# A mixture-of-experts stage whose narrow expert passes take fp32 weights unsplit, on the two column halves of the array

## What is computed

```python
def swiglu(h, w_gate, w_up, w_down):
    return (jax.nn.silu(h @ w_gate) * (h @ w_up)) @ w_down

def moe_swiglu(h, router_w, w_gate, w_up, w_down):
    logits = (h @ router_w).astype(jnp.float32)
    top_val, top_idx = lax.top_k(logits, TOP_K)
    top_w = jax.nn.softmax(top_val, axis=-1)
    gates = jnp.sum(jax.nn.one_hot(top_idx, N_EXPERTS, dtype=jnp.float32) * top_w[..., None], axis=-2)
    y = jnp.zeros_like(h)
    for e in range(N_EXPERTS):
        y = y + gates[..., e:e + 1] * swiglu(h, w_gate[e], w_up[e], w_down[e])
    return y
```

## Time and profile before

| | us |
|---|---|
| median of 3 runs | 1770.15 |
| lowest and highest | 1768.28, 1770.39 |
| profiled execution, first to last instruction (span) | 1766.1 |
| expert stage up to the M passes, from the first narrow product to the first M product | 745 to 1494 |
| M passes and end | 1494 to 1766 |

### The profile page before, as it was taken

The page is one execution under the profiler, slowest core; times in us unless marked ns, Lnnn a source line. Parts: engine busy times, 40 slices in busy tenths (PEclk is TensorE's granted clock), DMA queues, the critical chain, the costliest instruction groups (busy, mean ns, idle before and its releaser), DMA issues.

```text
span 1766.1 us, 25732 instructions
## 1 busy us (share of the span) xinstructions
PE 1692.1 (96%) x9921; PEld 1375.2 (78%) x9921; DVE 1364.1 (77%) x1225; ACT 1095.0 (62%) x1091; POOL 50.4 (3%) x100
## 2 busy tenths in 40 slices
PE   6999999899999999999899999999999999999997
PEld 4999999699999786667677776777677766788785
DVE  5666767576677687598698979897978888887886
ACT  2445544543333556587676877676867768767774
POOL 0200000001011000000000000000000000000000
PEclk9999999999999999899999999999999999999999
DMA  9975655268788440299799989998999899999993
GB/s 349 336 262 199 215 203 199 76 226 297 263 297 297 143 143 25 96 360 368 271 330 379 345 309 381 343 381 303 386 336 363 311 354 381 371 354 337 365 351 129
DMA packets 245612, 504.89 MB, mean 286 GB/s; under 512 B 11360, under 2 KB 83200, under 8 KB 245504
## 3 DMA queue, kind: packets, MB, share of 16 engines
q1 hardware_dynamic: 230224, 458.26, 72.1%
q0 software_dynamic: 12032, 43.00, 6.7%
q10 hardware_dynamic: 3248, 2.17, 0.4%
HBM read 502.34 MB, written 1.05 MB: 285 GB/s over the span
## 4 chain that ended last, share of the span: by engine, by line
PE 70%; DVE 16%; issue 7%; ACT 4%; DMA 1%; ACTq 0%; DVEq 0%; SPq 0%
PE ps L1410 18%; PE ps L1414 12%; DVE wlo L1618 10%; PE ps L1007 9%; PE ps L1011 9%; PE ps L1014 9%; PE ps L1458 3%; ACT whi L606 2%; PE ps L1388 2%; PE ps L1503 2%; PE ps L1062 1%; PE ps L1156 1%; PE ps L1180 1%; PE ps L1100 1%; DMA raw<-mod_w 1%
## 5 line engine op out<-in xcount | busy, mean ns | idle before, releaser
L1618 DVE TENSOR_TENSOR wlo<-raw,whi 128x2048 fp32r<-128x2048 f32 x428 | 967.8, 2288 | 245.9 <-ACT whi L606 241.0
L606 ACT ACTIVATE whi<-raw 128x2048 fp32r<-128x2048 f32 x428 | 807.8, 1913 | 196.1 <-PE ps L1011 81.9
L1410 PE MATMUL ps<-whi,ahi 128*128 128x512 f32 x896 | 297.7, 408 | 2.4 <-issue 1.8
L1414 PE MATMUL ps<-wlo,ahi 128*64 128x512 f32 (+1 forms) x896 | 259.0, 396 | 19.7 <-DVE wlo L1618 19.6
L1007 PE MATMUL ps<-ahi,whi 128*128 128x256 f32 x832 | 238.6, 287 | 1.7 <-DVE alo L1686 1.7
L1011 PE MATMUL ps<-alo,whi 128*128 128x256 f32 x832 | 235.8, 283 | 0.0
L1014 PE MATMUL ps<-ahi,wlo 128*128 128x256 f32 x832 | 235.7, 283 | 0.0
L1414 PEld LDWEIGHTS ps<-wlo,ahi 128*64 128x64 f32 (+1 forms) x896 | 136.5, 155 | 94.5 <-DVE wlo L1618 33.8
L1410 PEld LDWEIGHTS ps<-whi,ahi 128*128 128x128 f32 x896 | 165.9, 190 | 47.7 <-issue 11.2
L1007 PEld LDWEIGHTS ps<-ahi,whi 128*128 128x128 f32 x832 | 159.9, 192 | 5.1 <-issue 3.8
L1011 PEld LDWEIGHTS ps<-alo,whi 128*128 128x128 f32 x832 | 159.9, 192 | 0.3
(11 more groups left out here) (263 smaller groups left out, 2112.9 us busy)
## 6 DMA issues: line engine op xcount, KB each, us to landing
raw<-l_exp_w_gate SPq DMA_DIRECT2D x112, 1024.0 KB, 7.4
raw<-l_exp_w_up SPq DMA_DIRECT2D x112, 1024.0 KB, 7.9
raw<-l_exp_w_down SPq DMA_DIRECT2D x112, 1024.0 KB, 6.9
raw<-l_w_in SPq DMA_DIRECT2D x42, 1024.0 KB, 6.1
mraw<-mod_w POOLq DMA_DIRECT2D x80, 512.0 KB, 5.3
raw<-l_ffn_w_gate SPq DMA_DIRECT2D x14, 1024.0 KB, 5.1
raw<-l_ffn_w_up SPq DMA_DIRECT2D x14, 1024.0 KB, 6.5
raw<-l_ffn_w_down SPq DMA_DIRECT2D x14, 1024.0 KB, 5.7
```

Source lines behind the costliest of these rows:

```text
L606: act.activation(whi[s % SPL][:, :], raw[s % RAW][:, :], ACT.Copy).then_inc(hi_done, 1)
L1410: ins = pe.matmul(dst, stat, whi[s % SPL][:, a:a + BANK], start=start, stop=False, skip_group_check=True)
L1414: ins = pe.matmul(dst, stat, wlo[s % SPL][:, a:a + BANK], start=False, stop=stop, skip_group_check=True)
L1618: dve.tensor_tensor(wlo[s % SPL][:, :], raw[s % RAW][:, :], whi[s % SPL][:, :].bitcast(F32), ALU.subtract).then_inc(lo_done, 1)
```

## The change

Narrow passes stop splitting their weights. `as_landed` names the tiles of the narrow passes (`WHOLE`): all four gate and up tiles of a narrow step, and its two down tiles. `high` and `low` return at once for these tiles, and the numbering of split tiles (`split_at`) leaves them out.

- TensorE reads such a tile straight from `raw`, in fp32, with an fp32 stationary of 64 columns. `gate_beside_up` puts gate on columns and partitions 0 to 63 and up on 64 to 127 of one bank, product by product in turn. `down_halves` does the same with the two halves of the output's 1024 columns.
- SP refills a `raw` buffer that held such a tile when TensorE is done with it (`w_used`), not when DVE is, and it fetches gate and up tiles in turn.
- One copy (of one bank, now with gate and up) takes the place of two, and four transposes (`beside_T`) the place of the eight folding products. Gate is read by ACT and up by DVE from the turned bank, two 64-column blocks for each 128.
- The split of the hidden value and of the gathered activations goes, for narrow passes. The bank of gate and up alternates between 2 and 3 (`hidden_bank`).
- Wide and M passes keep their split tiles; the wide pass's fold writes in the new layout.

The core of the diff:

```diff
+            def raw_free(s, rr):
+                if s in WHOLE:
+                    sp.wait_ge(w_used, s + 1 + 6 * rr)
+                else:
+                    waits(sp, lo_done, split_at(s) + 1 + 6 * rr)
             def fetch(s, rr, src, dims):
-                waits(sp, lo_done, s - RAW + 1 + 6 * rr)
+                raw_free(s - RAW, rr)
...
             def high(s, rr=0):
+                if s in WHOLE:
+                    return
...
+            def gate_beside_up(q, b, s, k):
+                landed_whole(s)
+                landed_whole(s + 1)
+                for kk in range(4):
+                    kc = 4 * k + kk
+                    for half in range(2):
+                        ins = pe.matmul(half_bank(b, half), slots_of(q)[:, kc, :],
+                                        raw[(s + half) % RAW][:, kk * BANK:kk * BANK + BANK],
+                                        start=kc == 0, stop=kc == KC - 1, skip_group_check=True)
+                        if kk == 3:
+                            ins.then_inc(w_used, 1)
+            def down_halves(i, s, k):
+                landed_whole(s)
+                for kk in range(2):
+                    fc = 2 * k + kk
+                    for half in range(2):
+                        at = kk * D + half * BANK
+                        ins = pe.matmul(half_bank(0, half), sb_h[:, fc, :], raw[s % RAW][:, at:at + BANK],
+                                        start=i == 0 and fc == 0, stop=i == NF - 1 and fc == 3, skip_group_check=True)
+                ins.then_inc(w_used, 1)
+            def beside_T(n):
+                pe.wait_ge(gb_copied, n)
+                waits(pe, hb_done, n - 1)
+                for fc in range(4):
+                    ins = pe.transpose(bank(7, fc * P, fc * P + P), sb_g[:, fc * P:fc * P + P], ident)
+                ins.then_inc(tb_done, 1)
...
             def low(s, rr=0):
+                if s in WHOLE:
+                    return
```

More of the change, by code:

```diff
@@ L123, in gathers, with splits, as_landed @@
     return sum(has_a(kind) + has_b(kind) for kind in (PASSES + ("M",))[:q])
+def splits(q):
+    return sum({"L": 2, "M": 1, "S": 0}[kind] for kind in (PASSES + ("M",))[:q])
+def as_landed():
+    whole = set()
+    for n, (q, i) in enumerate(SEQ):
+        if PASSES[q] == "S":
+            whole.update(range(tile_of(q, i), tile_of(q, i) + 4))
+            whole.update(tile_of(*SEQ[n + 1]) + 4 + k for k in range(2))
+    return whole
 def tile_of(q, i):
@@ L129, in tile_of, with split_at, split_before, hidden_bank @@
     return M_MOE + max(6 * n - 2, 0)
+WHOLE = as_landed()
+SPLIT = [s for s in range(tile_of(NE + 1, 0) + 6 * NF) if s not in WHOLE]
+LOOPED = tile_of(FIRST_M, 1)
+def split_at(s):
+    return s - sum(w < s for w in WHOLE)
+def split_before(s):
+    return s - SPL if s >= LOOPED else SPLIT[split_at(s) - SPL]
+def hidden_bank(q, i):
+    n = SEQ.index((q, i))
+    return 2 + (n - 1 - max([m for m in range(n) if SEQ[m][0] == WIDE], default=-1)) % 2
 C_ID, C_ONE, C_UP, C_IOTA, C_DESC, C_EI, C_ORDER, C_SPILL = 0, 128, 256, 384, 512, 520, 528, 536
@@ L882, in gathered_part @@
                     act.wait_ge(gath, unit)
-                    waits(act, glo_done, unit - 1)
+                    waits(act, glo_done, splits(q))
                 for kc in kcs:
@@ L928, in step @@
                 high(s + 1 + SPL, rr)
-                if has_b(kind):
+                if q == WIDE:
                     act.wait_ge(w_used, s + 2)
@@ L1455, in folded_T @@
+            def folded_T(n, wide):
+                pe.wait_ge(ub_copied, wide)
                 waits(pe, hb_done, n - 1)
-                for at, half in ((0, sb_g), (4 * HP, sb_u)):
+                for at, half in ((0, sb_g), (HP, sb_u)):
                     for fc in range(4):
-                        ins = pe.matmul(bank(7, at + fc * HP, at + fc * HP + HP), half[:, fc * P:fc * P + P], fold,
+                        ins = pe.matmul(bank(7, at + fc * P, at + fc * P + HP), half[:, fc * P:fc * P + P], fold,
@@ L1520, in step @@
                 fold_before = None
-                if before is not None and has_b(PASSES[before[0]]):
+                if before is not None and before[0] == WIDE:
                     pe.wait_ge(gb_copied, steps_b(*before) + 1)
-                    fold_before = lambda: folded_T(steps_b(*before) + 1)
+                    fold_before = lambda: folded_T(steps_b(*before) + 1, before[1] + 1)
+                elif before is not None and has_b(PASSES[before[0]]):
+                    waits(pe, gb_copied, steps_b(*before) + (kind != "S"))
+                    fold_before = lambda: beside_T(steps_b(*before) + 1)
                 if i == 0:
-                    pe.wait_ge(glo_done, gathers(q + 1) + p)
+                    if kind == "S":
+                        pe.wait_ge(xg_done, gathers(q + 1))
+                    else:
+                        pe.wait_ge(glo_done, splits(q + 1) + p)
                 if has_a(kind):
@@ L1528, in step @@
                 added = 4 * wide_before(n - 1) if n else 0
-                waits(pe, yb_add, added - 3)
+                waits(pe, yb_add, added - 3 if kind != "S" else added - 5 + hidden_bank(q, i))
                 if q == WIDE:
@@ L1540, in step @@
                     middle()
-                waits(pe, yb_add, added - 2)
-                expert_tiles(q, 5, 3, s + 2, rr)
+                if kind == "S":
+                    gate_beside_up(q, hidden_bank(q, i), s + 2, 1)
+                else:
+                    waits(pe, yb_add, added - 2)
+                    expert_tiles(q, 5, 3, s + 2, rr)
                 if before is None:
@@ L2225, in _ @@
                 (0, 6): lambda: (turned_gates(0), gathered_low(WIDE), choose_slots(WIDE + 1)),
-                **{(WIDE, 2 * k): lambda k=k: gathered_low(WIDE + 1 + k) for k in range(4)},
                 (WIDE + 1, 0): lambda: choose_gates(WIDE),
```

183 lines of the change are left out of this document (99 added, 84 removed).

## The result

The changed kernel takes 1761.7 us by the median of five runs (1754.1 to 1763.3), the kernel before 1770.1 beside it: ratio 0.9943, 95% interval 0.9929 to 0.9958, so 0.6% faster. The forecast was 1740, 1.7% faster. Another series gave 1759.9 us and 0.995 (0.9937 to 0.9963). The profiled execution has a span of 1753.2 us, against 1766.1 before, and is near the short end of its runs.

What follows compares the result with a forecast made beforehand. TensorE and DMA were both taken as close to full, with DMA (394 GB/s) setting 16.0 us narrow steps. Terms -10.5, -19.3, -11.7, +3, +8 make -30.5: span 1735.6, plus 4 around it, said as 1740; own range 1722 to 1758.

Steps and rivals of the forecast that it cites:

- TensorE's narrow step: TensorE's work in a narrow step: paired fp32 products plus transposes, 11.2 us against 13.05 before.
- the copies, transposes and the hidden value's chain: Narrow steps, ACT and DVE: chain of about 1.5 us covered by the second gate and up pair; uncovered, 1.5 a step.
- The entry into M without split tiles: Start of M: nothing is split ahead, so 1.9 + 2.3 us of splitting stands bare, partly already now: +3 us.
- the ring costs more: Rival: behind each hold of raw buffers a lone issue lands in 8.1 us, not 5: +28, 1768 us; chance 0.11.
- The DMA did not go faster: Rival on tile transfers: DMA reaches 415 GB/s, 2.53 us a tile, giving 1718 us; chance 0.20.
- The clock did not cost 42 us in narrow steps: Rival: TensorE's clock falls in each narrow step, 35 x 1.2 = +42 us, wide steps +10: 1792; chance 0.14.
- The halves run side by side: Against a rival on narrow steps' column halves: serial products, 1910 us, or bare weight loads, 1789; chance 0.05.
- the ring's gaps: Cycles: raw buffers return late behind wide steps, idling DMA (first 4.5 us); cycles 87.9 and 68.4 us, six saving 19.3.
- Pass 0: Start to first wide step: 34 tiles at 2.66 us, 1.5 for irregularities; wide step at 848, not 858.49: -10.5 us.
- The clock: Start of wide steps: TensorE's clock low after waits for tiles, 1.1 us for each of seven: +8 us.
- Neither can save much more: Longer cycle: TensorE's own sum some 82 us, DMA's without gaps 79.8, against 87.9, so little more to save.
- What lies around the span: Time outside the profiled span, by the median of the runs: 4 us added to 1735.6.

Runs made afterwards that it cites:

- the two floors: Changed kernel, six raw buffers: half of narrow steps' gate and up products left out, 1735.8 us; separately, half of each narrow tile's transfer left out, 1675.7 us.
- the series kernel: Changed kernel with products reordered so that neighbours write the same column half, not in turns: 1791.8 us by one run.
- the second trace: Profiled execution of the unchanged changed kernel, timed again in another series: 1759.9 us, span 1756.2.
- the kernel with the filling: Changed kernel plus eight bf16 products of zeros between gate tile's arrival and up tile's wait, in narrow steps following two narrow steps: 1763.1 us against 1759.9.

## Why the prediction was off

**What held.** TensorE's narrow step: 11.2 forecast, 11.04 measured, and the halves side by side, as the two floors and the series kernel show. Narrow steps are set by tiles 2.66 us apart. One step of the changed kernel's pass 0, from one wait for `raw` to the next, and the stretch around it:

```profile
767.74 5.35 PE L1525 MATMUL ps<-raw,arena 128*64 128x512 f32 x16 [3.45 <-DMA raw<-l_exp_w_up]
...
783.71 5.35 PE L1525 MATMUL ps<-raw,arena 128*64 128x512 f32 x16 [3.01 <-DMA raw<-l_exp_w_up]
...
757.00:783.00 26.00, 20.04 (x84) 7.01 (x84) 3.62 (x18) 1.80 (x4) 0.00 (x0) 0.93 1.04 395
```

The step takes 15.97 us, forecast 16.0, at a share of 1.04 and 395 GB/s. No cost of the copies, transposes and the hidden value's chain shows. The entry into M without split tiles cost 1.5 of the 3 forecast. The rule of the Trainium skill ("TensorE: Matmul & The Clock Gate", Part 3), that a load overlaps only products of another row group, doesn't hold here: the loads lie two in 0.14 us, under products on the same rows. (The same part of the Trainium skill also names a load into the background weight buffer as one that is pulled ahead; no trace here tells whether these are such loads.)

**The rivals.** The measured 1761.7 lies between the forecast of 1740 and the 1768 of *the ring costs more*, nearer to the latter, and outside the forecast's own range of 1722 to 1758. That rival had the right place and a wrong reason: a lone issue lands in 4.9 us, not in 8.1. The DMA did not go faster (395 GB/s where it is full). The clock did not cost 42 us in narrow steps. The halves run side by side.

**What failed**, by the prediction's own steps, on spans: forecast -30.5, measured -12.9. Two terms were sized too small, the ring's gaps and the entry of M, and the clock's was sized too large and hid part of the first.

- *Pass 0: -10.5, measured -7.3 (and -4.4 in the second trace).* The step counted 34 tiles at 2.66 us behind one start. It left out that TensorE's gather for the wide pass now holds the ring as well; before, DVE released it. The gather sets the ring back by 1.8 us, and two single tiles land 1.3 us late each, 4.4 in all, where 1.5 was allowed. The gather, and the stretch of the DMA that follows:

```profile
821.05 7.26 PE L1454 MATMUL ps<-arena,xo 128*128 128x128 f32 x64
...
832.00:834.00 2.00, 2.00 (x12) 0.71 (x10) 0.00 (x0) 2.00 (x6) 0.00 (x0) 1.00 0.40 75
```

- *The ring's gaps: the term was too small.* The mechanism was right (the lead falls from nine tiles to six), the size not. The prediction gave the DMA 8.1 us without a tile in a long cycle and 4.6 in a short one. At full clock, in the kernel with the filling, the cycles take 89.8 and 69.7 us on average, so 10.0 and 5.9 us: 9.8 us more in six cycles (478.7 against 468.9). The first hold came out nearly as worked out (the wide step's first down tile issued 24.5 us into the cycle and landed at 29.4, forecast 24.2 and 29.2). What failed is the rule by which the rest was worked out, that a tile lands 5 us behind its issue or 2.66 behind the one ahead, whichever is later. SP's queue in the first long cycle, and the landing of the gate tile of 880.92:

```profile
875.65 2.22 SPq L502 DMA_DIRECT2D raw<-l_exp_w_down  x2
880.92 0.37 SPq L502 DMA_DIRECT2D raw<-l_exp_w_gate  x1
881.38 0.46 SPq L502 DMA_DIRECT2D raw<-l_exp_w_up  x1
886.88 0.37 SPq L502 DMA_DIRECT2D raw<-l_exp_w_gate  x1
...
raw<-l_exp_w_gate SPq DMA_DIRECT2D x1, 1024.0 KB, 6.9
```

The gate tile of 880.92 lands at 887.8, while the tile ahead of it landed at 883.7: 1.4 us later than both bounds. That of 886.88 takes 7.7 us and is 1.5 late. Where the forecast had gaps of 0.6 and 0.4, there are 1.4 and 1.5, and one of 0.5 ahead of them. Nor do "all buffers return in time" from the second step on: 1.0 us is missing once more 80 us into the cycle. Why a tile behind a nearly empty queue comes later than either bound isn't shown. In the third and fourth cycle the wide step began at the lower clock as well: its first twelve products took 4.4 us, not 2.8.
- *The clock: +8, measured 1.4 to 2.9 in the cycles, net of the filling's own cost.* Too large, and it hid the ring's error: without it the cycles would have been forecast at 468.9, against 478.7 at full clock.
- *"Neither can save much more".* The prediction worked out both floors, 79.8 for the DMA and 82 for TensorE, and the cycle at 87.9, and passed by the 4 to 6 us between as if they were little. They were the larger part of what the change has to give: two more tiles of lead won 49 of 58 us, 34.4 of them in the cycles.
- *M: +3, measured +10.8.* Of this 3.9 is a wait count that the changed numbering makes too high, which stood in the diff and wasn't worked through for the loop's second round, and 4.9 is the hidden value's split queued behind a tile that now lands late. That order was harmless as long as tiles lay ready (17.1 us for the same step before). The term itself, splitting that stands bare at the entry, was too large: 1.5 is left with both mended.
- *What lies around the span.* The forecast added 4 us. A run's time lies 1.7 us above its own span, before (1770.85 and 1769.1) as after (1754.88 and 1753.2); the rest of the 4 was that the profiled execution before was a short one. The changed kernel's median lies 7 us above its profiled run.

## What to carry to other kernels

Taking an engine out of the path of a buffer lengthens the time for which the buffer is held: count the lead in tiles before and after, and where it shrinks, look for idle memory in that stage before judging the change. Here the same edit gave 0.6% with six buffers and 3.3% with eight, while the buffers alone gave nothing. When tiles no longer lie ready, every queue with a fixed order shows its order: walk through each for what stands behind a wait for a tile, and each counter for the loop's second round.

## What was not expected of the hardware

fp32 products on two column halves with the same rows, written in turns, run fully at once: sixteen records in 3.6 us, pairs 0.43 us apart. When not written in turns, TensorE still lets products on the other half go ahead of three records that stand before them in the program: 5.35 us a pair rather than 6.9. The Trainium skill ("TensorE: Matmul & The Clock Gate", Part 2, step by step) says that products stay in program order and only loads are pulled ahead; the starts in the series kernel's trace say otherwise.
